# Splitting the value product of differential attention by halves of the keys, with filler matmuls around it

## Chip, cores, metric

One core of one Trainium2 chip runs the whole program. The metric is the device time of one execution in microseconds. The program is one inference step of a two-layer hybrid model in fp32; the change touches one stage of the first layer, a stretch of about 115 us of some 1,800.

## What is computed

Layer 0 has a differential attention with 4 heads. Each head has two query and two key vectors of 64 numbers per token, and one value vector of 128. There are 512 latent tokens (`x_sample`), which read 128 cached keys and their own 512 (640 in all), and 128 context tokens (`x_prompt`), which read only their own 128.

```python
def diff_attention_block(qb, k, v, lam):
    s = jnp.einsum('bqhcd,bkhcd->bhcqk', qb, k) * HEAD_DIM ** -0.5
    p = jax.nn.softmax(s, axis=-1)
    a = p[:, :, 0] - lam * p[:, :, 1]
    return jnp.einsum('bhqk,bkhe->bqhe', a, v)
```

The result is normalised per head, multiplied by a gain, and goes with the RG-LRU's output through the output projection. A router and 16 experts follow.

## The kernel before

The attention's work is cut into 20 items, `ITS = [(t, h) ...]`: query tile t of 128 tokens (0 to 3 latent, 4 context), head h. Items 0 to 15 have 640 keys, items 16 to 19 have 128. An item passes through these steps:

- TensorE `scores(i, c)` for c = 0 and 1: queries of 64 rows against the keys, into PSUM pair c. The operands of c = 0 lie on partitions 0 to 63, those of c = 1 on 64 to 127 (L1051, L1052; L1054 for context items).
- VectorE `maxes(i, c)` (L976), ScalarE `exps(i, c)` (L914, which frees the PSUM pair), VectorE `combine(i)` (L984, L985, L987), which makes one attention matrix of the two.
- TensorE `turn(i)` (L1081): 5 transposes into PSUM pair 2; ScalarE `turned(i)` (L355) copies them to `aT[i % 2]`.
- TensorE `rows(i)` (L1065): for each of 5 blocks of 128 keys one matmul with 128 rows of keys, added up in PSUM pair 3; VectorE `rows_out(i)` (L992) scales it into `osb` and frees pair 3.

Every fp32 matmul shows in the trace as two matmul instructions, a transpose as one. The loops of the three engines are written out by hand as one software pipeline. In round i, TensorE does `scores(i, 0)`, `turn(i - 2)`, `scores(i, 1)`, `rows(i - 3)`. VectorE does, in this order, `rows_out(i - 4)`, `maxes(i, 0)`, `combine(i - 1)`, `maxes(i, 1)`. ScalarE does `exps(i, 0)`, `turned(i - 2)`, `exps(i, 1)`. An engine works its instructions off in order, so one that waits on a semaphore holds up all behind it. `take(pe, name, pair)` makes TensorE wait until the last reader of that PSUM pair has released it.

At rounds 3, 7, 11, 15, 17 and 19 (`MOD_AT`) TensorE also does `late_mod_rows` (L486, 16 matmul instructions with 32 columns of weights each) and, a round later, `late_mod_turn` (L496); VectorE adds `late_mod_dve` (L514, L517). At every fourth round from 8 on, ScalarE squares (L874) and VectorE sums (L878) a finished tile.

After the loop VectorE applies the norm (L1010, L887, L888) tile by tile, and TensorE turns each tile (`dy_turn`, L1073); the output projection (`out_pe`, L222) starts after the last. `keep_busy` (L341) issues n matmuls of 128x128 by 128x512 whose results nobody reads. Three of them stand ahead of the first scores.

In layer 1, grouped-query attention runs its two heads of a pair on the two halves of the partitions: `scores(j, 0)` and `scores(j, 1)` stand directly one behind the other (L1794 and L1795, four matmul instructions for each head).

Of the kernel before, what the change touches and what calls it, by code (L numbers as in the profile page):

```python
# [18 lines left out]
ACT = mybir.ActivationFunctionType  # L19
# [3 lines left out]
P = 128  # L23
# [55 lines left out]
def build(nc, io, outs):  # L79
    with ExitStack() as ctx:  # L80
# [5 lines left out]
        def S(name):  # L86
            if name not in sems:
                sems[name] = ctx.enter_context(nc.semaphore("s_" + name))
            return sems[name]

        PSUM = ctx.enter_context(nc.psum_tensor("pairs", [P, 4, 1024], F32))
        pair_full = [S(f"pair_full{i}") for i in range(4)]
        pair_free = [S(f"pair_free{i}") for i in range(4)]
        units = Units()
# [28 lines left out]
        def ar(off, *shape):  # L123
            n = 1
            for x in shape:
                n *= x
            assert off + n <= AR, (off, n)
            v = arena[:, off:off + n]
            if len(shape) == 2:
                v = v.rearrange("p (a b) -> p a b", b=shape[1])  # L130
            elif len(shape) == 3:
                v = v.rearrange("p (a b c) -> p a b c", b=shape[1], c=shape[2])
            return v

        hflat = hT[:, :, :].rearrange("p k t -> p (k t)")
        rows = ar(0, NT, D)
# [21 lines left out]
        sps = sm[:, 200:208]  # L158
# [8 lines left out]
        def take(pe, name, pair=None):  # L167
            pair, n = units.add(name, pair)
            if n > 1:
                pe.wait_ge(pair_free[pair], n - 1)  # L170
            return PSUM[:, pair, :]

        def finish(ins, name):
            ins.then_inc(pair_full[units.of[name][0]], 1)


        def filled(eng, name):
            pair, n = units.of[name]
            eng.wait_ge(pair_full[pair], n)
            return PSUM[:, pair, :]  # L180

        def release(ins, name):
            ins.then_inc(pair_free[units.of[name][0]], 1)

        def emptied(eng, name):
            pair, n = units.of[name]
            eng.wait_ge(pair_free[pair], n)
# [8 lines left out]
        bank_of = lambda b: PSUM[:, b // 2, 512 * (b % 2):512 * (b % 2) + 512]  # L196
# [141 lines left out]
        def keep_busy(pe, ps, n):  # L338

            for _ in range(n):  # L340
                pe.matmul(ps[:, 0:512], ident, cst[:, 0:4, :].rearrange("p a b -> p (a b)"), start=True, stop=True)  # L341
# [12 lines left out]
        def copy(eng, dst, src):  # L354
            return eng.activation(dst, src, ACT.Copy) if eng is nc.scalar else eng.tensor_copy(dst, src)  # L355
# [122 lines left out]
        def late_mod_rows(pe, i, j):  # L478
            u = ("late", i)
            if j == 0:  # L480
                b_take(pe, u, 7)
                arrived(pe, all_mods[i])
            w, ps = chunk(all_mods[i]), bank_of(7)
            for q in range(4):
                k = 4 * j + q
                last = pe.matmul(ps[32 * q:32 * q + 32, :], csil[:, k, :], w[:, k, :], start=(j == 0), stop=(j == 1))  # L486
            if j == 1:
                b_finish(last, u)
                chunk_last[all_mods[i]] = u

        def late_mod_turn(pe, i, row):
            b_emptied(pe, ("late", i))
            u = ("late_turn", i)
            ps = b_take(pe, u, 7)
            for f in range(4):
                last = pe.transpose(ps[:, f * P:f * P + P], row[:, f * P:f * P + P], ident)  # L496
            b_finish(last, u)
# [349 lines left out]
        aT = [ar(8192 + 640 * i, T) for i in range(2)]  # L847
        osb = qkv[:, :, 0:512]
        ITS = [(t, h) for t in range(NT) for h in range(4)]
# [170 lines left out]
        def diff_pe(pe):  # L1020
            for tp in range(3):
                emptied(pe, ("pR", 0, 4, tp))
            pe.wait_ge(S("qk_rows"), 1)
            pe.wait_ge(S("late_here"), LATE_ALL)
            for h in range(4):
                u = ("kT", h)
                ps = take(pe, u)
                c = slice(h * P, h * P + P)
                pe.transpose(ps[:, 0:P], dk_c[:, c], ident)
                for t in range(NT):  # L1030
                    last = pe.transpose(ps[:, (t + 1) * P:(t + 2) * P], kr[:, t, c], ident)
                finish(last, u)
                u = ("qT", h)
                ps = take(pe, u)
                for t in range(NT):
                    last = pe.transpose(ps[:, t * P:t * P + P], qr[:, t, c], ident)
                finish(last, u)
            emptied(pe, ("kT", 2))
            keep_busy(pe, PSUM[:, units.of["kT", 2][0], :], 3)
            for h in range(4):  # L1040
                emptied(pe, ("kT", h))
                emptied(pe, ("qT", h))

            def scores(i, c):

                t, h = ITS[i]
                u = ("ds", i, c)
                ps = take(pe, u, c)
                q, k = qT[64 * c:64 * c + 64, h, t * P:t * P + P], kT[64 * c:64 * c + 64, h, :]
                if t < ST:  # L1050
                    pe.matmul(ps[:, 0:512], q, k[:, 0:512], start=True, stop=True)  # L1051
                    finish(pe.matmul(ps[:, 512:T], q, k[:, 512:T], start=True, stop=True), u)  # L1052
                else:
                    finish(pe.matmul(ps[:, 0:P], q, k[:, T:768], start=True, stop=True), u)  # L1054

            def rows(i):
                t, h = ITS[i]
                nk = NT if t < ST else 1
                u = ("do", i)
                ps = take(pe, u, 3)  # L1060
                emptied(pe, ("daT", i))
                for j in range(nk):
                    vals = vr[:, ST, h * P:h * P + P] if t == ST else \
                        dv_c[:, h * P:h * P + P] if j == 0 else vr[:, j - 1, h * P:h * P + P]
                    last = pe.matmul(ps[:, 0:P], aT[i % 2][:, j * P:j * P + P], vals, start=(j == 0), stop=(j == nk - 1))  # L1065
                finish(last, u)

            def dy_turn(t):
                pe.wait_ge(S("o_done"), t + 1)
                u = ("dyT", t)  # L1070
                ps = take(pe, u, t % 4)
                for h in range(4):
                    last = pe.transpose(ps[:, h * P:h * P + P], osb[:, t, h * P:h * P + P], ident)  # L1073
                finish(last, u)

            def turn(i):
                pe.wait_ge(S("d_comb"), i + 1)
                u = ("daT", i)
                ps = take(pe, u, 2)
                for j in range(NT if ITS[i][0] < ST else 1):  # L1080
                    last = pe.transpose(ps[:, j * P:j * P + P], pb[i % 2][:, 0, j * P:j * P + P], ident)  # L1081
                finish(last, u)


            pe.wait_ge(pair_free[3], units.uses[3])
            for i in range(len(ITS) + 3):
                if i < len(ITS):
                    scores(i, 0)
                if 0 <= i - 2 < len(ITS):
                    turn(i - 2)  # L1090
                if i - 1 in MOD_AT:
                    late_mod_turn(pe, MOD_AT[i - 1], mrow[MOD_AT[i - 1] % 2])
                if i < len(ITS):
                    scores(i, 1)
                if 0 <= i - 3 < len(ITS):
                    rows(i - 3)
                if i in MOD_AT:
                    late_mod_rows(pe, MOD_AT[i], 0)
                    late_mod_rows(pe, MOD_AT[i], 1)
            pe.wait_ge(bank_free[7], banks.uses[7])  # L1100
            for t in range(NT):
                dy_turn(t)

# [139 lines left out]
                release(copy(act, grow[:, g, :], filled(act, u)), u)  # L1243

        def route_act(act, step, l):
            for t in range(NT):
                u = ("hr", l, t)
                release(copy(act, hrow[:, t, :], filled(act, u)), u)
                if t == 0:
                    act.wait_ge(S("lg_sub"), l + 1)  # L1250
                    act.activation(lg, lg, ACT.Exp).then_inc(S("lg_exp"), 1)
            if l == 1:
                act.wait_ge(S("h_stored"), 32)
                for t in range(NT):
                    u = ("xr", t)
                    release(copy(act, xrow[:, t, :], filled(act, u)), u)
# [1326 lines left out]
        def _(act):  # L2583
            step = Steps(act, S("act_step"))
            setup_act(act, step)
            for l in range(2):
# [35 lines left out]
                norm_root_act(act, l, 1)  # L2622
                norm_shift_act(act, l, 1)
                route_act(act, step, l)
                moe_act_run(act, l)
                if l == 0:
# [126 lines left out]
```

## Time and profile before

| | us |
|---|---|
| three runs | 1799.83, 1801.79, 1792.06 |
| median | 1799.83 |
| the profiled execution | 1796.14 |
| its span (first to last instruction) | 1794.2 |
| TensorE busy | 1606.8 (90%) |
| VectorE busy | 645.0 (36%) |
| ScalarE busy | 441.5 (25%) |

The span is the time of the profiled execution but for 1.9 us around it. Busy shares are means over stages with different limits; what counts for the change is what happens between 304 and 424 us of the span. "PEclk" is the TensorE clock granted, 1.00 for 2.4 GHz and 0.50 for 1.2 GHz.

### The profile page before, as it was taken

The page shows a single profiled execution, that of the slowest core. Times are in us where ns is not written, and L with a number is a line of the kernel's source. Part 1 is how long each engine was busy: PE and PEld are TensorE (multiplying, and loading weights), DVE is VectorE, ACT ScalarE, POOL GpSimd, SP SyncE. Part 2 cuts the span into 40 slices and gives each one's busy share as a digit, 9 for nine tenths or more (in the row PEclk, how much of TensorE's full clock was granted, in tenths as well). Part 3 has the DMA queues.
Part 4 walks back from the last instruction along what each step waited for, and adds up shares of the span by engine and source line. Part 5 has one row for each costly group of instructions (what it writes and reads, how often), then busy time and mean ns, then how long its engine had stood idle before and what let it go on. Part 6 is the DMA issues. An engine that isn't in the chain of part 4 may idle for free.

```text
span 1794.2 us, 37806 instructions
## 1 busy us (share of the span) xinstructions
PE 1606.8 (90%) x16674; PEld 1031.5 (57%) x16674; DVE 645.0 (36%) x1300; ACT 441.5 (25%) x744; POOL 239.6 (13%) x237
## 2 busy tenths in 40 slices
PE   5999975998949999998999989988889959999992
PEld 2554433664526776764555558667675537776761
DVE  5234466562270000003129636634462270000003
ACT  4111175451031111112110246432231032111100
POOL 0000000000001111100000026156540001111103
PEclk8999997898979999999999999999999989999996
DMA  9832281235127999996112100011115127999994
GB/s 345 295 122 94 100 292 43 94 123 206 50 103 275 376 379 381 384 392 195 47 53 89 50 1 1 1 49 50 49 50 199 65 88 264 372 384 381 384 395 138
DMA packets 90318, 330.07 MB, mean 184 GB/s; under 512 B 10708, under 2 KB 16456, under 8 KB 82024
## 3 DMA queue, kind: packets, MB, share of 16 engines
q1 hardware_dynamic: 76016, 287.29, 42.1%
q0 software_dynamic: 9168, 32.65, 6.6%
q10 hardware_dynamic: 5032, 8.65, 1.3%
q8 instruction: 79, 1.29, 0.3%
q14 instruction: 23, 0.19, 0.0%
HBM read 303.79 MB, written 24.78 MB: 183 GB/s over the span
## 4 chain that ended last, share of the span: by engine, by line
PE 82%; DVE 9%; DMA 3%; ACT 3%; issue 2%; ACTq 0%; POOL 0%; DVEq 0%
PE pairs L222 27%; PE pairs L1342 16%; PE pairs L1354 12%; PE pairs L1051 2%; PE pairs L1325 2%; PE pairs L1065 1%; PE pairs L341 1%; PE pairs L1811 1%; PE pairs L1831 1%; PE pairs L1794 1%; PE pairs L2038 1%; PE pairs L486 1%; PE pairs L2049 1%; PE pairs L1179 1%; DMA ring<-in_w_in_ab 1%
## 5 line engine op out<-in xcount | busy, mean ns | idle before, releaser
L222 PE MATMUL pairs<-hT,ring 128*128 128x128 f32 (+1 forms) x1120 | 306.2, 436 | 2.2 <-ACT hT L355 2.2
L222 PEld LDWEIGHTS pairs<-hT,ring 128*128 128x128 f32 x1120 | 170.3, 192 | 139.0 <-issue 139.0
L355 ACT ACTIVATE arena<-pairs 128x512 f32<-128x512 f32 (+6 forms) x208 | 120.9, 600 | 423.2 <-PE pairs L222 201.6
L222 PE MATMUL pairs<-ring,hT 128*128 128x512 f32 (+1 forms) x448 | 177.4, 557 | 0.0
L1342 PEld LDWEIGHTS pairs<-arena,ring 128*64 128x64 f32 x4096 | 143.1, 137 | 15.9 <-issue 15.9
L1342 PEld LDWEIGHTS pairs<-arena 128*64 128x64 f32 x4096 | 142.9, 137 | 13.8 <-issue 13.7
L1342 PE MATMUL pairs<-arena,ring 128*64 128x80 f32 x4096 | 146.3, 233 | 2.4 <-issue 2.4
L1342 PE MATMUL pairs<-arena 128*64 128x80 f32 x4096 | 145.8, 233 | 2.0 <-ACT arena L1377 1.0
L222 PEld LDWEIGHTS pairs<-ring,hT 128*128 128x128 f32 x448 | 84.8, 190 | 92.1 <-issue 89.1
L1410 DVE TENSOR_SCALAR hT<-pairs,arena 80x512 f32<-80x512 f32 x32 | 23.9, 747 | 272.0 <-ACT hT L1386 272.0
L1354 PE MATMUL pairs<-ring,arena 128*80 128x512 f32 x256 | 112.7, 593 | 0.2 <-DMA ring<-in_exp_w 0.2
L1354 PE MATMUL pairs<-arena 128*80 128x512 f32 x256 | 112.5, 592 | 0.0
L1406 DVE TENSOR_TENSOR arena<-hT,pairs 128x160 f32<-128x160 f32 x64 | 20.5, 321 | 249.0 <-PE pairs L1342 249.0
L355 DVE COPY arena<-pairs 128x512 f32<-128x512 f32 (+7 forms) x37 | 25.2, 704 | 188.8 <-PE pairs L222 181.4
L1437 POOL DMA_INDIRECT moe_rows<-hT,arena x32 | 45.5, 1421 | 295.0 <-DVE hT L1410 295.0
L1386 ACT ACTIVATE hT<-pairs,arena 80x512 f32<-80x512 f32 x32 | 21.9, 684 | 212.8 <-PE pairs L1354 212.8
L1354 PEld LDWEIGHTS pairs<-ring,arena 128*80 128x80 f32 x256 | 37.6, 152 | 63.1 <-issue 62.9
L1354 PEld LDWEIGHTS pairs<-arena 128*80 128x80 f32 x256 | 37.8, 153 | 62.6 <-issue 62.6
L1140 DVE SCALAR_TENSOR_TENSOR xT<-pairs,modt,xT 128x512 f32<-128x512 f32 x24 | 18.0, 750 | 139.4 <-PE pairs L222 125.7
L1377 ACT ACTIVATE arena<-pairs 128x640 f32<-128x640 f32 x32 | 22.5, 704 | 183.8 <-PE pairs L1325 183.8
L341 PE MATMUL pairs<-cst 128*128 128x512 f32 x126 | 59.4, 615 | 3.2 <-DVE hT L1410 1.7
L1427 POOL DMA_INDIRECT hT<-h_rows,arena x32 | 29.4, 919 | 237.5 <-PE pairs L1325 197.8
(386 smaller groups left out, 2150.3 us busy)
## 6 DMA issues: line engine op xcount, KB each, us to landing
arena<-in_exp_w SPq DMA_DIRECT2D x48, 2048.0 KB, 18.3
ring<-in_exp_w SPq DMA_DIRECT2D x48, 2048.0 KB, 20.1
ring<-in_w_mod SPq DMA_DIRECT2D x24, 2048.0 KB, 8.2
ring<-in_w_in_ab SPq DMA_DIRECT2D x5, 2048.0 KB, 11.6
ring<-in_w_in_cd SPq DMA_DIRECT2D x5, 2048.0 KB, 7.8
ring<-in_w_out SPq DMA_DIRECT2D x4, 2048.0 KB, 7.7
moe_rows<-arena POOLq DMA_DIRECT2D x2, 2560.0 KB, 14.5
h_rows<-arena POOLq DMA_DIRECT2D x2, 2560.0 KB, 8.4
```

The costliest lines, as they stand in the source:

```text
L222: last = pe.matmul(out, lhs(k), rhs(k), start=(k == 0), stop=(k == KD - 1))
L341: pe.matmul(ps[:, 0:512], ident, cst[:, 0:4, :].rearrange("p a b -> p (a b)"), start=True, stop=True)
L355: return eng.activation(dst, src, ACT.Copy) if eng is nc.scalar else eng.tensor_copy(dst, src)
L1051: pe.matmul(ps[:, 0:512], q, k[:, 0:512], start=True, stop=True)
L1325: last = pe.transpose(ps[:, o:o + CAP], xe[par][:, k::KD], ident[0:CAP, 0:CAP])
L1342: last = pe.matmul(lin_of(j, f)[c:c + 64, :], w[:, k, f * P + c:f * P + c + 64], rhs, start=(k == 0), stop=(k == KD - 1))
L1354: last = pe.matmul(PSUM[0:CAP, 3, 512 * half:512 * half + 512], hid[par][:, f, :], w2[:, f, 512 * half:512 * half + 512], start=(f == 0), ...
L1377: act.activation(xeT[par], ps, ACT.Copy).then_inc(pair_free[0], 1)
L1386: act.activation(ye[par][:, 0:512], PSUM[0:CAP, 3, 0:512], ACT.Copy, scale=gateT[:, bass.ds(i, 1)])\
L1410: v.tensor_scalar(ye[par][:, 512:1024], PSUM[0:CAP, 3, 512:1024], gateT[:, bass.ds(i, 1)], None, ALU.mult).then_inc(pair_free[3], 1)
L1427: g.indirect_dma_start(xe[e % 2], None, DR["h", l], off(e)).then_inc(S(f"gathered{e % 2}"), 16)
L1437: g.indirect_dma_start(DR["m", l], off(e), ye[e % 2], None, compute_op=ALU.add)\
```

## The change

`rows(i)` is split into `rows(i, 0)` and `rows(i, 1)`. Half 0 takes the rows 64 to 127 of each block of 128 keys and stands ahead of `scores(i, 0)`, whose operands lie on partitions 0 to 63. Half 1 takes the rows 0 to 63 and stands behind `scores(i, 1)`, whose operands lie on 64 to 127. Both add into the same PSUM bank; half 1 waits until half 0 has finished (`d_half`). The wait for PSUM pair 3 (`rows_out` of the item before) and for `aT` now stands with half 0, at the head of the round. Each half has as many matmuls as the whole had. Fillers are added in rounds 0 and 1 and ahead of the `dy_turn`s. In `route_act` an `Exp` on one column is added ahead of the copies.

```diff
-            def rows(i):
+            def rows(i, half):
...
-                ps = take(pe, u, 3)
-                emptied(pe, ("daT", i))
+                r = slice(64 - 64 * half, 128 - 64 * half)
+                if half == 0:
+                    take(pe, u, 3)
+                    emptied(pe, ("daT", i))
+                else:
+                    pe.wait_ge(S("d_half"), i + 1)
...
-                    last = pe.matmul(ps[:, 0:P], aT[i % 2][:, j * P:j * P + P], vals, start=(j == 0), stop=(j == nk - 1))
-                finish(last, u)
+                    last = pe.matmul(PSUM[:, 3, 0:P], aT[i % 2][r, j * P:j * P + P], vals[r], start=(half == j == 0),
+                                     stop=(half == 1 and j == nk - 1))
+                if half == 1:
+                    finish(last, u)
+                else:
+                    last.then_inc(S("d_half"), 1)
...
             pe.wait_ge(pair_free[3], units.uses[3])
+            pe.wait_ge(pair_free[2], units.uses[2])
             for i in range(len(ITS) + 3):
+                if 0 <= i - 3 < len(ITS):
+                    rows(i - 3, 0)
                 if i < len(ITS):
                     scores(i, 0)
                 if 0 <= i - 2 < len(ITS):
                     turn(i - 2)
+                if i < 2:
+                    keep_busy(pe, PSUM[:, 2, :], 3 if i == 0 else 2)
                 if i - 1 in MOD_AT:
                     late_mod_turn(pe, MOD_AT[i - 1], mrow[MOD_AT[i - 1] % 2])
                 if i < len(ITS):
                     scores(i, 1)
                 if 0 <= i - 3 < len(ITS):
-                    rows(i - 3)
+                    rows(i - 3, 1)
                 if i in MOD_AT:
                     late_mod_rows(pe, MOD_AT[i], 0)
                     late_mod_rows(pe, MOD_AT[i], 1)
             pe.wait_ge(bank_free[7], banks.uses[7])
+            keep_busy(pe, bank_of(7), 3)
             for t in range(NT):
                 dy_turn(t)
...
         def route_act(act, step, l):
+            act.activation(sps[:, 6:7], sps[:, 0:1], ACT.Exp)
             for t in range(NT):
```

## Rows read from the trace of the kernel before

**Rows 1.** The page's part 4, the chain that ended last, shares of the span by engine.
```profile
PE 82%; DVE 9%; DMA 3%; ACT 3%; issue 2%; ACTq 0%; POOL 0%; DVEq 0%
```

**Rows 2.** Windows: stretch, its length, busy us of each engine, granted clock, DMA.
```profile
308.07:328.55 20.48, 18.96 (x56) 10.79 (x60) 8.75 (x16) 7.69 (x18) 0.00 (x0) 0.50 0.00 1
328.55:390.78 62.23, 62.23 (x345) 39.30 (x337) 39.58 (x84) 31.21 (x65) 0.00 (x0) 1.00 0.30 102
410.47:424.12 13.65, 10.14 (x26) 5.62 (x27) 6.70 (x12) 2.97 (x6) 0.00 (x0) 0.50 0.35 122
1117.02:1127.26 10.24, 8.80 (x101) 6.89 (x101) 5.53 (x21) 5.79 (x19) 4.90 (x7) 1.00 0.00 1
```

**Rows 3.** The chain in order of time, rounds 6 to 8: start, us, what.
```profile
338.80 1.05 PE pairs L1051 x2
...
340.08 0.69 PE pairs L1081 x5
...
342.05 1.31 PE pairs L1065 x10
343.36 1.05 PE pairs L1051 x2
...
347.91 1.85 PE pairs L486 x16
```

**Rows 4.** Timeline of one round: start, us, engine, line, form, [idle before <- releaser].
```profile
343.29 1.12 PE L1051 MATMUL pairs<-arena 64*128 64x512 f32 x2
343.40 0.35 DVE L992 TENSOR_SCALAR arena<-pairs,sm 128x128 f32<-128x128 f32 x1 [0.41 <-PE pairs L1065]
...
344.74 0.82 DVE L976 TENSOR_REDUCE sm<-pairs 128x1 f32<-128x640 f32 x1 [0.99 <-PE pairs L1052]
...
345.48 0.15 DVE L984 RECIPROCAL sm<-sm 128x2 f32<-128x2 f32 x1
...
345.92 0.88 DVE L987 SCALAR_TENSOR_TENSOR arena<-arena,sm 128x640 f32<-128x640 f32 x1
...
346.73 0.82 DVE L976 TENSOR_REDUCE sm<-pairs 128x1 f32<-128x640 f32 x1
...
356.88 0.18 DVE L514 TENSOR_REDUCE sm<-pairs 128x8 f32<-128x32 f32 x1
...
357.58 0.17 DVE L984 RECIPROCAL sm<-sm 128x2 f32<-128x2 f32 x1
```

**Rows 5.** The chain in order of time, from the fillers to item 4.
```profile
302.37 2.58 PE pairs L341 x6
304.95 1.07 PE pairs L1051 x4
...
307.60 0.89 ACT arena L914 x2
...
308.53 2.29 PE pairs L1051 x4
...
329.26 1.05 PE pairs L1051 x2
```

**Rows 6.** Timeline of grouped-query attention in layer 1, both heads' scores.
```profile
1072.72 1.14 PE L1794 MATMUL pairs<-arena 64*128 64x512 f32 x4
1073.68 0.39 PE L1795 MATMUL pairs<-arena 64*128 64x128 f32 x4
```

**Rows 7.** The chain, from the context items to the output projection.
```profile
390.78 0.42 PE pairs L1054 x2
...
394.05 0.42 PE pairs L1054 x2
...
409.30 0.35 DVE arena L992
...
419.53 30.62 PE pairs L222 x101
```

**Rows 8.** Timeline of the routing in layer 0, ScalarE's table and TensorE behind it.
```profile
513.16 1.28 ACT L1251 ACT_TABLE_LOAD   x1
...
515.97 0.71 PE L1200 MATMUL pairs<-cst,arena 128*16 128x128 f32 x5
```

## Prediction

> **What bounds the kernel now.** I read the page first. The chain that ended last runs over TensorE for 82% of the span [rows 1], so time taken from TensorE's path anywhere comes off the end, unless another engine takes the place. Then I looked at the attention stage by windows. From 328.55 to 390.78 us, rounds 4 to 15, TensorE is busy for 62.23 of 62.23 us at clock 1.00; VectorE has 39.58 busy us of them, ScalarE 31.21 [rows 2]. Ahead of that lie 20.48 us at clock 0.50. The chain in order of time gives the price of a round: 4.56 us from 338.80 to 343.36, all TensorE, made of scores of 1.28 us (338.80 to 340.08) twice, turn 0.69, product 1.31 [rows 3]. A modulation adds 1.85 for its rows [rows 3]. Rounds 4 to 15 take 390.78 - 329.26 = 61.5 us [rows 5, 7], so the three modulations in them cost (61.5 - 12 x 4.56) / 3 = 2.3 us each, rows and turn.
>
> **The split itself, on TensorE.** Ten product instructions become twenty, ten in each half. The trace has no 64-row product, but it has two groups of matmuls on different halves of the partitions. In layer 1 four L1794 start within 1.14 us, and the L1795 of both heads start only behind them, at 1073.68; all eight are over in little more than the 1.28 us of a single head here [rows 6, 3]. Item 0 shows the same: four L1051 in 1.07 us of the chain, the time of two [rows 5, 3]. So halves do run side by side, and instructions of the second half pass three that wait in the first. The edit asks for more: scores(i, 0) stands behind ten. If they pass as freely, a half product beside its scores costs the longer of 1.31 and 1.28, and TensorE's round becomes 1.31 + 0.69 + 1.31 = 3.31 us, 1.25 less than 4.56. Over 12 rounds that would be 15 us.
>
> On this point the Trainium skill ("TensorE: Matmul & The Clock Gate", Part 3, What overlaps and what doesn't) speaks against the change: matmuls are said to start and end strictly in program order, and only weight loads to overlap across row groups. The trace does not agree with it for four instructions, since the second head's wide matmuls start ahead of the first head's narrow ones [rows 6]. For ten no run here shows either. By the rule a scores would begin about when the last of ten products does; that is the first rival below.
>
> **The wait that moves.** The saving does not reach the end, because `take` on pair 3 moves from the foot of the round to its head. Before, product i-3 waited at the end of round i for rows_out(i-4), which VectorE had done at the round's start: no wait shows. Now round i on TensorE begins with half 0 of i-3, which waits for rows_out(i-4); VectorE does that only behind maxes(i-1, 1), which itself needs scores(i-1, 1). Behind the waiting instruction stand scores(i, 0), turn(i-2) and scores(i, 1), and for scores(i, 0) waits VectorE. That closes a loop through both engines. Its legs, from the timeline of a round [rows 4]: rows_out 0.35 plus 0.04 to the next engine; first score to its maximum 344.74 - 343.29 = 1.45; maximum to combine 345.48 - 344.74 = 0.74; L984 to L987 345.92 - 345.48 = 0.44; L987 to the next maximum 346.73 - 345.92 = 0.81; that maximum 0.74. Sum 4.57 us. The way over TensorE is as long: 0.39 + 1.31 (half 0 beside the first scores) + 0.69 + 1.45 + 0.74 = 4.58. I take 4.59 for the handover between the two. So a round costs what it cost before, 4.56, and TensorE is idle for some 1.2 us of it.
>
> Rounds 4 to 15 after: 12 x 4.59 = 55.1. A modulation's rows now lie over the wait of 0.74 + 0.39 = 1.13, which makes 2.3 - 1.13 = 1.2 each, but VectorE's sums for it (356.88 to 357.58, 0.70 [rows 4]) come onto the loop: 1.9 x 3 = 5.6. Two row sums L878, by L976 about 0.7 each: 1.4. Together 62.1 against 61.5, **0.6 lost**.
>
> **The first rounds.** Between 306.3 and 308.5 us TensorE waits for the first exponentials, and from 308.07 the clock is 0.50 [rows 5, 2]. Round 4 begins at 329.26. With the fillers, at 2.58 us for six instructions [rows 5]: scores(0, 0) 304.95 to 306.2; three fillers to 308.8; scores(0, 1) and (1, 0) side by side to 310.1; two fillers (4/6 of 2.58 = 1.7) to 311.8. The exponential of (0, 1) follows its maximum: 308.80 + 1.45 + 0.86 = 311.1 (0.86 is 0.82 and the 0.04), and an exponential frees its pair after 0.89 + 0.04 = 0.93 [rows 5], at 312.0. scores(1, 1) then 312.0; maximum and exponential again, 3.24 in all, scores(2, 1) at 315.3, to 316.5. ScalarE's copy of turn(0) ends by then; half 0 and scores(3, 0) to 318.0, turn 318.7, scores(3, 1) 320.0, modulation 321.8. Round 4 begins at 321.8 against 329.26: **7.4 saved**, all of it the clock; the five fillers delay nothing that the exponentials don't. If the clock stayed at 0.50 there, the fillers would cost 4.3 us more instead. It should hold: the fillers are the same instructions that stood at 1.00 ahead of 304.95, and later a round has 3.3 of 4.6 us busy, 72%, where a stretch of layer 1 kept 1.00 with 8.80 of 10.24 [rows 2]. That is near, not the same.
>
> **The context items.** In rounds 16 to 18 the products of items 13 to 15 are full size, but the scores beside them take 0.42 [rows 7]. A round there is 0.42 + 0.69 + 0.42 + 1.31 = 2.8 before, and 1.31 + 0.69 + 1.31 + 0.39 = 3.7 after: 0.9 x 3 = 2.7, of which some 0.6 lies under waits for ScalarE. The last three items each add a second small product and the wait, about 0.4: 1.1. From 390.78 to the last rows_out, 409.65, it is 18.9 us now; **3.2 lost**. Bounds: 1.5 (all three under other waits) and 4.5.
>
> **Output turns.** From 410.47 to 424.12 the clock is 0.50 and the projection starts in it at 419.53 [rows 2, 7]: 4.6 us at half speed, worth 2.3, and the last turn 0.6. Three fillers end about when the first turn is due; the turns behind them fill little, so the clock may fall again before the projection. Between 0 and 2.9 I take **1.4 saved**.
>
> **The Exp in route_act.** It moves a table load of 1.28 us [rows 8] ahead of the router's exponential. TensorE does turns up to 515.97, when it goes on without a wait, and ScalarE has long finished. Worth 0 in both layers. Without that cover it would be worth 1.3 in each.
>
> **Sum.** 7.4 - 0.6 - 3.2 + 1.4 = 5.0 us. Against its own time, 1796.14, that is 1791.1; against the median of the runs, 1799.83, it is **1794.8**. Behind this stage TensorE carries the chain to the end of the layer, so the 5 us arrive. A measurement here tells about 0.5%, 9 us, from no change.
>
> **Rivals.** (a) *Ten queued products hold the scores back.* Scores then start behind nine of them, 9 x 0.13 = 1.2 us later (1.31 for ten [rows 3]), in the 13 rounds from 3 to 15: +16: 1811. Any delay over 5.0 / 15 = 0.33 us a round makes the kernel slower than before. For it: nothing here passes more than three. Against: rows 6. Chance 0.13.
> (b) *A half product costs more than a whole one,* because its weight loads don't hide under 64-row matmuls. At twice the price, 2.6 us, the way over TensorE is 0.39 + 2.6 + 0.69 + 2.6 = 6.3 a round, 1.7 more, 22 us in 13 rounds: 1817. Against: the narrow scores in rows 6, four in 0.39 us. Chance 0.04.
> (c) *The clock falls to 0.50 in the first rounds in spite of the fillers:* 7.4 saved becomes about 4 lost: 1806. Chance 0.1.
> (d) *The loop isn't there,* that is, rows_out is never late. Then a round is TensorE's 3.3 or VectorE's 3.1, with handovers 3.5, and 13 us more come off: 1782. It would take another order of VectorE's work than the code has. Chance 0.12.
> My forecast has 0.61; its own range, by the bounds of the parts and the runs' own spread, is 1788 to 1802. With (a), (c) and (d) inside, the range is 1781 to 1812. Faster by over 0.5%: (d) and the lower edge of the forecast, 0.22. Slower: (a), (b) and part of (c), 0.2. Within: 0.58.
>
> **What would show it.** Right: clock 1.00 from 301 to about 400; rounds of 4.6 us with TensorE busy some 3.3 and idle about 1.2 ahead of L1065, released by DVE L992; L1051 starting with L1065, not behind it; context rounds longer by 0.9. Wrong: rounds of 3.5 (d), maxima later than 1.5 us behind the first L1065 (a), half products over 1.4 (b), half clock after 308 (c).

## The result and the profile after

The changed kernel takes 1818.18 us (median of 4 runs, 1816.33 to 1823.77) against 1797.94 for the kernel before (4 runs, 1792.06 to 1801.79): ratio 1.0121 [1.0084, 1.0158], 1.2% slower. The forecast was 1795, range 1781 to 1812: 5 us saved were forecast, and 20 are lost. The profiled execution took 1816.33 us, span 1813.8.

The chain's shares by engine (page, part 4, changed kernel) show more of VectorE and of transfers than before, and less of TensorE [rows 1]:

```profile
PE 78%; DVE 10%; DMA 6%; ACT 3%; issue 2%; ACTq 0%; POOL 0%; DVEq 0%; SPq 0%
```

They don't place the loss: the kernel called scores first below has 78%, 10% and 6% too and isn't slower than before, and split only has 81%, 10% and 3% and is slower still.

To place the time I cut the stage at four events that every kernel here has: the first scores (L1051), the first maximum of item 4 and of item 16 (L976), the last rows_out (L992), and the first instruction of the output projection (L222). The same cut serves for the experiments below; us, from the profiled executions, the last column the half-clock stretches that begin in the stage, summed ("three ahead" and the others are told of below; columns are rounded one by one):

| kernel | scores 0 to item 4 | item 4 to 16 | item 16 to last rows_out | to projection | stage | at half clock |
|---|---|---|---|---|---|---|
| before | 25.8 | 60.7 | 18.0 | 10.2 | 114.7 | 34.1 |
| changed | 20.0 | 79.6 | 20.1 | 9.8 | 129.5 | 27.3 |
| scores first | 18.5 | 58.5 | 21.2 | 9.8 | 108.0 | 6.8 |
| one product ahead | 18.5 | 62.1 | 21.9 | 9.8 | 112.2 | 10.2 |
| three ahead | 19.1 | 68.7 | 21.2 | 9.8 | 118.8 | 17.1 |
| fillers only | 19.5 | 60.7 | 18.0 | 9.8 | 107.9 | 6.8 |
| split only | 24.3 | 83.7 | 21.0 | 10.2 | 139.3 | 64.9 |
| rows_out early | 20.0 | 62.3 | 20.1 | 9.8 | 112.1 | 3.4 |
| filler each round | 20.0 | 71.8 | 21.0 | 9.8 | 122.6 | 13.7 |
| open loop | 18.5 | 51.1 | 20.9 | 9.8 | 100.3 | 3.4 |
| open loop, no fillers | 20.5 | 51.1 | 20.8 | 10.2 | 102.6 | 23.9 |

The stage is 14.8 us longer, of the 19.6 by which the spans of before and after differ. Ahead of the stage it is 0.5 us less. What follows the stage took 1374.7 us before and 1379.9 after; over all the kernels of the table it scatters between 1372.3 and 1384.4, so nothing is read from those 5 us. The loss sits in one column: rounds 4 to 15, +18.9.

Windows of the changed kernel (stretch, length, busy us, granted clock), to lay beside [rows 2]:

```profile
304.46:324.42 19.96, 19.46 (x105) 10.98 (x105) 10.33 (x19) 9.92 (x20) 0.00 (x0) 1.00 0.05 8
324.42:404.04 79.62, 65.82 (x456) 49.95 (x456) 39.11 (x84) 31.17 (x65) 0.00 (x0) 0.85 0.23 79
353.27:366.01 12.74, 8.28 (x67) 6.59 (x67) 7.84 (x19) 5.52 (x12) 0.00 (x0) 1.00 0.18 68
366.50:383.73 17.23, 14.15 (x117) 10.24 (x116) 9.71 (x21) 7.89 (x18) 0.00 (x0) 1.00 0.35 123
383.73:400.80 17.07, 15.42 (x70) 12.23 (x74) 5.48 (x13) 4.27 (x10) 0.00 (x0) 0.50 0.01 1
404.04:424.20 20.16, 17.90 (x139) 11.96 (x138) 10.29 (x41) 9.46 (x28) 0.00 (x0) 1.00 0.58 207
```

The first rounds run at 1.00 where they ran at 0.50. In rounds 4 to 15 TensorE is idle for 13.8 of 79.6 us, and the clock is 0.85 on average: 3.4 us at half from 335.9, 3.4 from 342.8, and 17.1 from 383.7. VectorE and ScalarE did the same work as before (39.11 and 31.17 against 39.58 and 31.21), so neither has become the bound by its load.

One round of the changed kernel at full clock, its timeline (start, us, engine, line, form, [idle before <- releaser]), beside [rows 4]:

```profile
360.66 0.48 PE L1070 MATMUL pairs<-dv_c,arena 64*128 64x128 f32 x2 [2.52 <-DVE arena L992]
360.98 0.72 PE L1070 MATMUL pairs<-arena 64*128 64x128 f32 x5
361.44 0.69 PE L1051 MATMUL pairs<-arena 64*128 64x512 f32 x1
361.54 0.50 PE L1070 MATMUL pairs<-arena 64*128 64x128 f32 x3
...
362.71 0.76 PE L1090 MATMUL pairs<-cst,arena 128*128 128x128 f32 x5
362.89 0.82 DVE L976 TENSOR_REDUCE sm<-pairs 128x1 f32<-128x640 f32 x1 [2.28 <-PE pairs L1052]
...
363.63 0.15 DVE L984 RECIPROCAL sm<-sm 128x2 f32<-128x2 f32 x1
...
364.07 0.89 DVE L987 SCALAR_TENSOR_TENSOR arena<-arena,sm 128x640 f32<-128x640 f32 x1
...
364.88 0.82 DVE L976 TENSOR_REDUCE sm<-pairs 128x1 f32<-128x640 f32 x1
365.61 0.34 DVE L992 TENSOR_SCALAR arena<-pairs,sm 128x128 f32<-128x128 f32 x1
366.01 0.48 PE L1070 MATMUL pairs<-dv_c,arena 64*128 64x128 f32 x2 [1.21 <-DVE arena L992]
```

The half products are L1070, the turn L1090. The round is 366.01 - 360.66 = **5.35 us**, against 4.56 [rows 3] and a forecast of 4.59. Walk the loop. L992 releases TensorE, 0.40 (365.61 to 366.01). The first score starts at 361.44, not at 360.66: **0.78 us behind the first half product**, when seven of the ten have started and three are left (0.78 in each of the ten rounds 4 to 13, all at full clock where the scores start; at half clock it is 1.45, 384.14 to 385.59, again behind seven). Score to maximum 361.44 to 362.89: 1.45. Maximum to L984 0.74, to L987 0.44, to the next maximum 0.81, to L992 0.73. The sum is 5.35. Every leg is the forecast's but the 0.78, which the forecast had at nothing.

The chain in order of time shows the first rounds and, in the second fence, the rounds at half clock (the first stretch answers to [rows 5]):

```profile
304.46 1.05 PE pairs L1051 x2
...
305.74 2.77 PE pairs L341 x6
308.51 1.07 PE pairs L1051 x4
...
322.24 0.97 PE pairs L1070 x7
```

```profile
384.14 1.86 PE pairs L1070 x7
...
393.02 1.86 PE pairs L1070 x7
...
402.59 0.97 PE pairs L1070 x7
```

Round 4 begins at 322.24 (forecast 321.8, before 329.26). At 384.14 and 393.02 the seven half products that go ahead of the scores take 1.86 us where they took 0.97 to 1.04: such rounds are 8.88 and 9.57 us long (the second with a modulation).

### The profile page after: what moved, and what is told of

It is laid out like the page before. It is cut to its first block, busy times and chain, and to the rows that moved or that the text cites. A ratio compares the mean times of both kernels' runs of the same rounds, so it can differ in the third digit from the quotient of the medians.

```text
span 1813.8 us, 38176 instructions
## 1 busy us (share of the span) xinstructions
PE 1614.2 (89%) x16858; PEld 1045.3 (58%) x16858; DVE 645.7 (36%) x1300; ACT 441.9 (24%) x746; POOL 239.0 (13%) x237
## 3 DMA queue, kind: packets, MB, share of 16 engines
q8 instruction: 80, 1.31, 0.3%
## 4 chain that ended last, share of the span: by engine, by line
PE 78%; DVE 10%; DMA 6%; ACT 3%; issue 2%; ACTq 0%; POOL 0%; DVEq 0%; SPq 0%
PE pairs L222 26%; PE pairs L1358 14%; PE pairs L1370 11%; DMA ring<-in_exp_w 3%; PE pairs L1070 2%; PE pairs L1341 2%; PE pairs L341 1%; PE pairs L1827 1%; PE pairs L1847 1%; PE pairs L2054 1%; PE pairs L1810 1%; PE pairs L1051 1%; PE pairs L486 1%; PE pairs L2065 1%; DMA ring<-in_w_in_ab 1%
## 5 line engine op out<-in xcount | busy, mean ns | idle before, releaser
L222 PE MATMUL pairs<-hT,ring 128*128 128x128 f32 (+1 forms) x1120 | 303.9, 434 | 2.2 <-ACT hT L355 2.2
L222 PEld LDWEIGHTS pairs<-hT,ring 128*128 128x128 f32 x1120 | 169.6, 191 | 137.3 <-issue 137.3
L222 PE MATMUL pairs<-ring,hT 128*128 128x512 f32 (+1 forms) x448 | 177.4, 557 | 0.0
L1358 PEld LDWEIGHTS pairs<-arena 128*64 128x64 f32 x4096 | 142.9, 137 | 14.0 <-issue 13.8
L222 PEld LDWEIGHTS pairs<-ring,hT 128*128 128x128 f32 x448 | 84.9, 190 | 92.0 <-issue 89.0
L1426 DVE TENSOR_SCALAR hT<-pairs,arena 80x512 f32<-80x512 f32 x32 | 23.9, 747 | 275.9 <-ACT hT L1402 275.9
L341 PE MATMUL pairs<-cst 128*128 128x512 f32 x142 | 69.3, 632 | 3.2 <-DVE hT L1426 1.7
```

The lines of the kernel that those rows point to most:

```text
L222: last = pe.matmul(out, lhs(k), rhs(k), start=(k == 0), stop=(k == KD - 1))
L1358: last = pe.matmul(lin_of(j, f)[c:c + 64, :], w[:, k, f * P + c:f * P + c + 64], rhs, start=(k == 0), stop=(k == KD - 1))
L1426: v.tensor_scalar(ye[par][:, 512:1024], PSUM[0:CAP, 3, 512:1024], gateT[:, bass.ds(i, 1)], None, ALU.mult).then_inc(pair_free[3], 1)
```

## The experiments

**Scores first.** The changed kernel with the two calls at the head of a round swapped, so nothing queues ahead of the scores; the wait for rows_out stays.

```
-                if 0 <= i - 3 < len(ITS):
-                    rows(i - 3, 0)
                 if i < len(ITS):
                     scores(i, 0)
+                if 0 <= i - 3 < len(ITS):
+                    rows(i - 3, 0)
```

> The changed kernel with one order turned: in each round scores(i, 0) goes first and half 0 of the product behind it, so the scores neither stand behind ten queued product instructions nor behind the wait for rows_out. Theory (the scores are held 0.77 us behind seven of the ten products, and the wait for rows_out stands ahead of them): the round of 5.35 us falls by about 0.8 to 0.9, TensorE is busier and keeps clock 1.00 from 384 to 401 us; the stage ends some 13 to 20 us earlier than in the changed kernel, total 1788 to 1805. Rival (the clock alone is at fault, the order isn't): rounds of the same length wherever the clock is 1.00, total 1810 or more.

Measured: 1795.71 us against 1794.30, 0.9995 [0.9973, 1.0017]. Its chain in order of time:

```profile
351.81 0.35 DVE arena L992
352.20 1.38 PE pairs L1070 x10
353.58 0.69 PE pairs L1090 x5
...
355.66 0.82 DVE sm L976
356.48 0.27 DVE arena L992
356.79 1.38 PE pairs L1070 x10
```

A round is 356.79 - 352.20 = 4.59 us: L992 still releases half 0, but the first scores are no longer in the loop; it runs half product 1.38, turn 0.69, second scores to their maximum 1.39, then that maximum and L992, 1.13 with the handover. This one swap takes back all that the changed kernel had lost. It takes the queue away and shortens the round, after which the clock never falls in rounds 4 to 15; so by itself it doesn't separate the two.

**One product ahead, three ahead.** The half product is cut so that one product (two instructions), or three (six), stand ahead of the scores and the others behind them. The wait stays at the head in both.

```
-            def rows(i, half):
+            def rows(i, half, a=0, b=5):     # blocks a to b
...
                 if 0 <= i - 3 < len(ITS):
-                    rows(i - 3, 0)
+                    rows(i - 3, 0, 0, 1)     # three ahead: 0, 3
                 if i < len(ITS):
                     scores(i, 0)
+                if 0 <= i - 3 < len(ITS):
+                    rows(i - 3, 0, 1, 5)     # three ahead: 3, 5
```

> The changed kernel, but only the first of half 0's five matmuls (two instructions) ahead of scores(i, 0), the other four behind them. The wait for rows_out stays at the head of the round. Theory (a group passes a few instructions that wait in the other group, but not ten): the first scores start within 0.1 us of the first product instruction in place of 0.77, the round falls from 5.35 to about 4.6, and the total to 1795 to 1808. Rival (matmuls start strictly in program order, or the whole delay is the wait): the distance from first product to first scores stays above 0.2 us for the second pair of instructions and the total hardly moves.

> The changed kernel with three of half 0's five matmuls (six instructions) ahead of scores(i, 0), two behind. It measures how many queued instructions the scores can pass. In the changed kernel the first scores start with the seventh of ten, 0.77 us after the first; with two ahead they start together. Theory (three may wait, not more): they start with the third, 0.2 to 0.4 us after the first, and plain rounds are 4.8 to 4.9 us. Rival (any number below a larger queue passes freely): within 0.05 us, rounds 4.6. Rival (the count doesn't matter, only the order): 0.6 us or more.

Measured: one ahead 1799.11 against 1794.30, 1.0021 [0.9997, 1.0045]; three ahead 1811.36 in a single run, and so no interval. TensorE's timeline with one product ahead:

```profile
368.93 0.37 PE L1070 MATMUL pairs<-dv_c,arena 64*128 64x128 f32 x1 [1.20 <-DVE arena L992]
368.93 0.69 PE L1051 MATMUL pairs<-arena 64*128 64x512 f32 x1
...
369.14 0.27 PE L1070 MATMUL pairs<-dv_c,arena 64*128 64x128 f32 x1
```

And with three ahead:

```profile
368.76 0.49 PE L1070 MATMUL pairs<-dv_c,arena 64*128 64x128 f32 x2
369.09 0.27 PE L1070 MATMUL pairs<-arena 64*128 64x128 f32 x1
369.10 0.69 PE L1051 MATMUL pairs<-arena 64*128 64x512 f32 x1
```

With two instructions ahead the score starts in the same moment as the product that waited, 0.00 us; with six, 0.34 later, behind three; with ten, 0.78 later, behind the seven L1070 that the chain counts. In both, three are left when the score starts. It is so in each of the rounds 4 to 15: 0.33 or 0.34 us, behind three, with three matmuls ahead, and at most 0.01 with one. The wait alone (one ahead: rows_out in the loop, no queue) gives rounds of 4.59 us, as forecast, by two products of its chain:

```profile
331.87 0.37 PE pairs L1070
...
336.15 0.27 DVE arena L992
...
336.46 0.37 PE pairs L1070
```

Rounds 4 to 15 take 62.1 us, with one half-clock stretch of 3.4 us inside. Laid beside them by the first maxima of the items, the five rounds that are at full clock in both kernels are 0.73 to 0.77 us longer in the changed kernel: that is the price of the queue. With three ahead every round without extras touches a half-clock stretch, so the expected 4.8 to 4.9 us can't be read; rounds at full clock in both are 0.44 to 0.45 shorter than the changed kernel's, as 0.78 - 0.34 asks.

**Fillers only, split only.** The two halves of the change apart: the kernel before with the fillers of both places, and the changed kernel without them.

```
             pe.wait_ge(pair_free[3], units.uses[3])
+            pe.wait_ge(pair_free[2], units.uses[2])
...
                     turn(i - 2)
+                if i < 2:
+                    keep_busy(pe, PSUM[:, 2, :], 3 if i == 0 else 2)
...
             pe.wait_ge(bank_free[7], banks.uses[7])
+            keep_busy(pe, bank_of(7), 3)
```

> The kernel before with the fillers alone (three and two in rounds 0 and 1, three ahead of the output turns), product whole. Theory (the fillers save the half clock of 308 to 328 us, and the split alone loses): clock 1.00 through the first rounds, round 4 begins 7 to 9 us earlier, total 1787 to 1793 (before: 1798). Rival (the fillers' time eats what the clock gives): 1795 to 1800.

> The changed kernel without the fillers. Theory (fillers worth 7 to 9 us in the changed kernel too): first rounds at half clock, total 1822 to 1830. Rival (TensorE has so much idle time in its rounds now that the clock falls anyway and the fillers are worth nothing): 1816 to 1820.

Measured: fillers only 1792.63, 0.9987 [0.9969, 1.0005]; split only 1822.36 against 1794.30, 1.0144 [1.0104, 1.0184]. The slowdown belongs to the split. Windows of the kernel with fillers only, its first rounds and the start of the projection:

```profile
305.60:325.10 19.50, 18.76 (x85) 9.79 (x85) 10.57 (x19) 9.92 (x20) 0.00 (x0) 1.00 0.04 3
413.50:420.00 6.50, 6.50 (x8) 2.67 (x9) 0.00 (x0) 0.00 (x0) 0.00 (x0) 0.53 1.01 381
```

The first rounds keep 1.00 and take 6.3 us less than in the profile of before; the projection still starts at half clock. Yet the median is only 1.7 us lower, and the interval holds no change. That the other executions of before didn't lose those 6 us would explain it, but the mean granted clock of whole executions speaks against that: it is 0.955 in the median of the 29 of before and 0.960 in that of the 12 with fillers. So with fillers most executions did gain clock somewhere, and why the time hardly followed stays open.

**rows_out early.** The changed kernel with VectorE's rows_out(i-3) ahead of the second maxima instead of behind them, which takes one maximum out of the loop and leaves queue and wait.

```
-                if 0 <= i - 4 < len(ITS):
-                    rows_out(i - 4)
                 if i < len(ITS):
                     maxes(i, 0)
...
                     combine(i - 1)
+                if 0 <= i - 3 < len(ITS):
+                    rows_out(i - 3)
                 if i < len(ITS):
                     maxes(i, 1)
```

> The changed kernel, but VectorE does rows_out(i) ahead of the second maximum of its round instead of behind it; TensorE's order is untouched. Theory (the round is a loop: last scores, maximum, rows_out, half 0, scores held 0.77 us, maximum, combine): the leg of the maximum, 0.74 us, leaves the loop, rounds without extras fall from 5.35 to 4.6 to 4.7 us, total 8 to 14 us under the changed kernel's 1818, so 1804 to 1810. Rival (the wait for rows_out costs nothing, all is the queue): rounds stay at 5.3 and the total at 1815 or more.

Measured: 1796.88 against 1795.64, 1.0013 [0.9996, 1.0030]. Its timeline and its window of rounds 4 to 15:

```profile
356.11 0.82 DVE L976 TENSOR_REDUCE sm<-pairs 128x1 f32<-128x640 f32 x1 [0.96 <-PE pairs L1052]
...
356.85 0.15 DVE L984 RECIPROCAL sm<-sm 128x2 f32<-128x2 f32 x1
...
357.30 0.89 DVE L987 SCALAR_TENSOR_TENSOR arena<-arena,sm 128x640 f32<-128x640 f32 x1
...
358.12 0.35 DVE L992 TENSOR_SCALAR arena<-pairs,sm 128x128 f32<-128x128 f32 x1
...
358.59 0.46 PE L1070 MATMUL pairs<-dv_c,arena 64*128 64x128 f32 x2 [0.57 <-DVE arena L992]
```

```profile
324.90:387.20 62.30, 55.58 (x456) 41.74 (x456) 38.93 (x85) 30.88 (x65) 0.00 (x0) 1.00 0.29 101
```

L992 follows L987 directly and still releases the half product, 0.47 later. From the half product before, at 353.88, it is 0.78 to the scores (354.66), 1.45 to their maximum, then 0.74 + 0.45 + 0.82 + 0.47: 4.71 us, the changed kernel's loop less one maximum. The time came in under the 1804 to 1810 expected: in this profile the clock never fell in this stretch. (Shorter rounds alone don't ensure that; with one product ahead, at 4.59 us a round, it fell once.) That makes it the ruler for the clock, as far as single profiles of two kernels can be one. Laid beside it, position by position, the changed kernel's rounds at full clock are longer by 0.7 in the mean (5.35 against 4.71, 5.70 against 5.00; two of the others by 1.3 and by nothing), 8.4 in 12 rounds, while the four that hold a half-clock stretch are longer by 2.3, 1.6 and, the two from 384.14 to 402.59 together, 18.45 - 11.02 = 7.4: 11.3, of which 2.8 is the same 0.7 a round and some **8.5 the clock**, an estimate. 8.4 + 8.5 = 16.9 of the 17.3 between the two kernels.

**A filler each round.** The changed kernel with one dummy matmul at the foot of rounds 4 to 19 that have no modulation in or ahead of them: the loop stays as it is, TensorE has less idle time.

```
+                if 4 <= i < len(ITS) and i not in MOD_AT and i - 1 not in MOD_AT:
+                    pe.wait_ge(bank_free[7], banks.uses[7])
+                    keep_busy(pe, bank_of(7), 1)
```

> The changed kernel with one more filler matmul (two instructions, 0.86 us) at the foot of rounds 4 to 19 that have no modulation work, where TensorE waits about 1.2 us for rows_out. Theory (of the changed kernel's loss some 6 to 9 us is half clock, at 336 to 346 and at 384 to 401 us, which comes from idle time in the rounds): the clock holds, plain rounds stay at 5.35, total 1808 to 1813. Rival (the falls of the clock don't matter, or fillers can't hold it): 1815 to 1820.

Measured: 1809.08 against 1795.64, 1.0084 [1.0060, 1.0108]. The changed kernel's ratio was 1.0121 [1.0084, 1.0158], and the intervals touch, so the totals alone don't show the gain; the profile of the stage does. Window of rounds 4 to 15:

```profile
324.00:395.60 71.60, 64.87 (x467) 45.97 (x466) 38.75 (x84) 31.21 (x65) 0.00 (x0) 0.95 0.25 86
```

The stretch falls from 79.6 to 71.8 us with the useful work unchanged and the clock at 0.95: most of the 8.5 us that the clock had taken. What stays, 71.8 against 60.7, is the long round and what two half-clock stretches of 3.4 us still cost. The two losses are thus separate: the clock's was mostly removed with the long round in place.

**Open loop, with and without fillers.** Scores first and rows_out early together: neither the queue nor a late rows_out is left. Then the same without all fillers.

> Both turned: scores(i, 0) ahead of half 0, and rows_out ahead of the second maximum. Theory (neither queue nor wait holds the scores; TensorE's work of 1.3 + 0.7 + 1.3 us a round and the short wait for rows_out bound it): plain rounds of 3.8 to 4.0 us against 4.56 whole, the stage some 6 to 9 us shorter than with scores first alone, total 1782 to 1790. Rival (VectorE's own work and the context rounds eat it, or the clock falls with the idle time): rounds of 4.3 or more, total 1791 to 1797.

> The version with both orders turned (scores first, rows_out ahead of the second maximum), without any filler. Theory (the fillers keep the first rounds at clock 1.00 and are worth some 5 us; the well-ordered split is worth the rest): the clock is 0.50 in part of the first rounds, total 1785 to 1790 against 1783 with fillers and 1795 before. Rival (only split and fillers together gain, since the split's idle time lets the clock fall without them): 1792 or more.

Measured: **1782.92 against 1795.64, 0.9942 [0.9924, 0.9959]**, faster than both kernels; without the fillers 1783.58 against 1793.11, 0.9941 [0.9923, 0.9959]. The chain in order of time of the open loop, and its window of rounds 4 to 15:

```profile
347.94 0.86 PE pairs L1051 x2
...
349.02 0.80 PE pairs L1070 x8
349.82 0.69 PE pairs L1090 x5
350.52 0.32 PE pairs L1051
...
351.84 0.86 PE pairs L1051 x2
```

```profile
324.30:375.40 51.10, 51.10 (x448) 40.51 (x449) 39.72 (x84) 30.63 (x65) 0.00 (x0) 1.00 0.35 124
```

The round is 351.84 - 347.94 = 3.90 us, all of it TensorE, and the stretch is 9.6 us shorter than before. So the split does what it should: it gives 0.66 us a round once no wait eats it. (No run turned the two orders in the unsplit kernel; there TensorE was busy for 62.23 of 62.23 us [rows 2], so they had no wait to remove.) It gives 3.90, not the 3.31 of a perfect overlap. The second half beside its scores takes 1.32 us (350.52 to 351.84), as put in the forecast; the first takes 1.88 (347.94 to 349.82), since the product, behind four instructions of the scores, runs on for 0.80 after they are done. Without fillers 10.2 us of the first rounds ran at half clock:

```profile
305.00:330.00 25.00, 22.18 (x136) 15.42 (x134) 14.72 (x30) 12.32 (x26) 0.00 (x0) 0.80 0.21 77
```

Its stage is 2.3 us longer for it (102.6 against 100.3), and the ratios can't tell the two apart; the 5 us expected of the fillers don't show.

## Why the prediction was wrong

**The step that failed first** is "If they pass as freely". The rows it stood on had three waiting instructions, and three is what the scores pass: with two, six and ten ahead they start 0.00, 0.34 and 0.78 us late. Rival (a) had the mechanism, at 1.2 us a round; measured 0.78. Its 1811 comes nearer to the measured time than it earned: with 0.78 in its 13 rounds it would be 1805, and the rest is the clock and what follows the stage. (Its threshold of 5.0 / 15 = 0.33 a round should have divided by the same 13: 0.38.) The sizes in the forecast's chain of steps otherwise held, so the round is 4.57 + 0.78 = 5.35. Without the moved wait the 0.78 might have lain under TensorE's idle time; in this kernel it sits in the loop, because the half product at the head waits for rows_out, and the scores queue behind it. The Trainium skill ("TensorE: Matmul & The Clock Gate", Part 3, What overlaps and what doesn't), by which matmuls start and end in program order, warned of this. The traces agree with it in part: a scores' matmul does start ahead of the products issued before it, which the rule excludes, but of three at most, and behind the others it keeps its order.

**The step that failed second** is "It should hold", the clock: the sum for rounds 4 to 15 has it at nothing. It held in the first rounds, of which rival (c) was the doubt, and fell in the later ones, which had been put at 72% busy in rounds of 4.6 us and came to be 65% in one stretch of longer rounds, still at 1.00, and 82% in the next, after which the clock went to 0.50. Some 8.5 us, in no step and no rival.

**The wait that moves** was right: the loop through rows_out exists, one product ahead shows it at 4.59 us. That its twelve rounds take 62.1 us, the forecast's figure, is partly luck, since a half-clock stretch that the forecast didn't have is in them. Rival (d), no loop, is refuted for this order of work. The open loop gave 3.90 us a round where (d) had 3.5. **The half product** was right by itself: ten in 1.38 us against 1.31, and rival (b) falls. That it costs beside its scores only the longer of the two held for the second half (1.32 us in the open loop) and not for the first (1.88 against 1.31).

**The smaller terms.** First rounds: round 4 begins 7.0 us earlier, 0.5 of that from ahead of the stage, so 6.5 saved, forecast 7.4. Context items: 20.1 against 18.0 us, 2.1 lost, forecast 3.2, bounds 1.5 to 4.5. Output turns: 10.2 became 9.8, as with fillers alone: 0.4 saved, forecast 1.4; the clock fell again before the projection. The Exp in route_act: in the timeline of the changed kernel its exponential and TensorE behind it are

```profile
525.32 0.27 ACT L1267 ACTIVATE arena<-arena 128x80 f32<-128x80 f32 x1
...
528.08 0.71 PE L1215 MATMUL pairs<-cst,arena 128*16 128x128 f32 x5
```

From the start of the turns that cover it (523.10) L1215 comes after 4.98 us; before it was 4.99. Worth 0 in layer 0, as forecast.

**The sum by columns.** -5.8 + 18.9 + 2.1 - 0.4 = 14.8 us in the stage (the first column ends at item 4's maximum, which the queue already delays, so it shows 5.8 and not 6.5). Of the 18.9, 0.78 x 12 = 9.4 is the queue, some 8.5 the clock; 1 is left, near the 0.6 that the forecast lost here.

**Open.** Why fillers alone bring 6 us in the profile and 1.7 in the medians; what made the clock fall at 383.7 and not in the idler stretch before (TensorE had waited for 2.3 us, from 381.84 to 384.14, but ahead of 360.66 for 2.5); and whether the changed kernel's other 5 us lie in the scatter of single executions. No kernel was run with exactly three or four instructions ahead, so "three" rests on starts in runs with two, six and ten. The division of the loss into queue and clock rests on one profile of each kernel.

## What to carry to other kernels

When an accumulator's wait moves to the head of a round, walk the whole loop through the other engine, and move the release forward with it: here the same split was 1.2% slower with the wait closed into a loop and 0.6% faster with it open. To run two groups of matmuls side by side, put the one that the other engine waits for first, or put only an instruction or two ahead of it. A round with idle time on TensorE can cost twice, by its length and then by the clock, and fillers gave back most of the second part and none of the first.

## What the runs showed of the hardware

Matmuls on one half of the partitions started ahead of up to three waiting ones on the other half, in the same moment as the first of them (368.93 and 368.93), and no further: 0.34 us late with six ahead, 0.78 with ten.

The granted clock did not follow the busy share in a simple way: TensorE was busy for 8.28 of 12.74 us and kept 1.00, then for 14.15 of 17.23, and then the clock was 0.50 for 17.1 us, in which it was busy for 15.42. The two half-clock stretches of 3.4 us there, 6.9 us apart, were worth 1.6 and 0.9 us by the comparison with rows_out early, an estimate.
